# Experts ranked by row count on the chip, with one weight fetch each and blocks of 128 or 64 slots

## What is computed

```python
def _hier_moe(h, w_rg, b_rg, w_re, b_re, w1, w3, w2):
    ...
    g_top = jnp.argmax(g_logits, axis=-1)
    ...
    top_v, top_j = lax.top_k(e_in, TOP_K_EXPERTS)          # 2 of the 4 experts of the group
    w_sel = jax.nn.softmax(top_v, axis=-1) * gate_g
    e_id = g_top[:, None] * EXPERTS_PER_GROUP + top_j
    ...
    for e in range(N_EXPERTS):                              # 16
        he = jax.nn.silu(hf @ w1[e]) * (hf @ w3[e])
        y = y + combine[:, e:e + 1] * (he @ w2[e])
```

## Time and profile before

| | |
|---|---|
| median of three timed runs | 1888.61 us |
| span of the profiled execution | 1885.4 us |
| TensorE busy | 1815.4 us (96%) |
| VectorE busy | 1446.7 us (77%) |
| ScalarE busy | 982.6 us (52%) |
| GpSimd busy | 118.2 us (6%) |
| moved by DMA | 417.14 MB, mean 221 GB/s |

### The profile page before, as it was taken

One profiled execution on the slowest core, in us unless ns is written; L12 is line 12 of the kernel. 1 busy time (PEld: TensorE's weight loads), 2 busy tenths in 40 slices (PEclk: granted clock), 3 DMA queues, 4 the chain that ended last, 5 costly groups with the idle time before them and its releaser, 6 DMA issues.

```text
span 1885.4 us, 28170 instructions
## 1 busy us (share of the span) xinstructions
PE 1815.4 (96%) x10912; PEld 1597.0 (85%) x10912; DVE 1446.7 (77%) x1543; ACT 982.6 (52%) x932; POOL 118.2 (6%) x116
## 2 busy tenths in 40 slices
PE   7999999999999999999999999998998899999998
PEld 6888899998888788889999978886997777777876
DVE  7555786857877765567877687779588889999998
ACT  4444465534444454446464345443435456767774
POOL 1000000000000000000000000001000011212222
PEclk9999999999999999999999999998999999999999
DMA  6555455564777465545546557774432359999995
GB/s 250 190 188 196 161 179 179 201 224 144 280 252 259 157 216 185 200 156 181 199 164 245 176 186 279 248 260 144 140 136 90 103 185 373 367 373 391 389 385 217
DMA packets 61615, 417.14 MB, mean 221 GB/s; under 512 B 7288, under 2 KB 7664, under 8 KB 13648
## 3 DMA queue, kind: packets, MB, share of 16 engines
q1 hardware_dynamic: 51392, 369.19, 54.4%
q0 software_dynamic: 10112, 46.59, 7.3%
q10 hardware_dynamic: 16, 0.01, 0.0%
HBM read 405.79 MB, written 9.98 MB: 221 GB/s over the span
## 4 chain that ended last, share of the span: by engine, by line
PE 80%; DVE 11%; DVEq 3%; issue 3%; ACT 1%; ACTq 1%; DMA 0%; POOL 0%; POOLq 0%
PE ps L1916 14%; PE ps L1915 7%; PE ps L1900 7%; PE ps L1902 7%; PE ps L1901 7%; PE ps L2017 4%; PE ps L2018 4%; PE ps L2021 4%; PE ps L899 3%; PE ps L897 3%; PE ps L898 3%; PE ps L926 2%; PE ps L1913 2%; DVE wlo L2350 2%; PE ps L928 2%
## 5 line engine op out<-in xcount | busy, mean ns | idle before, releaser
L2350 DVE TENSOR_TENSOR wlo<-raw,whi 128x2048 fp32r<-128x2048 f32 x236 | 538.2, 2289 | 194.0 <-ACT whi L2182 191.2
L2182 ACT ACTIVATE whi<-raw 128x2048 fp32r<-128x2048 f32 x236 | 451.1, 1912 | 271.6 <-PE ps L1902 112.7
L1916 PE MATMUL ps<-xT,whi 128*128 128x512 f32 x1232 | 440.4, 397 | 0.0
L1915 PE MATMUL ps<-xT,wlo 128*128 128x256 f32 x1232 | 344.6, 280 | 0.1
L1916 PEld LDWEIGHTS ps<-xT,whi 128*128 128x128 f32 x1232 | 231.9, 188 | 47.6
L1900 PE MATMUL ps<-xT,whi 128*128 128x256 f32 x928 | 263.5, 284 | 2.0 <-DVE xT L2361 2.0
L1901 PE MATMUL ps<-xT,whi 128*128 128x256 f32 x928 | 263.2, 284 | 0.0
L1902 PE MATMUL ps<-xT,wlo 128*128 128x256 f32 x928 | 263.1, 284 | 0.0
L1915 PEld LDWEIGHTS ps<-xT,wlo 128*128 128x128 f32 x1232 | 233.0, 189 | 8.9 <-DVE xT L2369 1.0
L1544 DVE TENSOR_TENSOR wlo<-raw,whi 128x2048 fp32r<-128x2048 f32 x76 | 201.3, 2661 | 10.6 <-ACT whi L1124 9.9
L2206 ACT ACTIVATE rest<-ps 128x512 f32<-128x512 f32 x88 | 52.7, 599 | 251.9 <-PE ps L1916 251.9
(11 more groups left out here) (516 smaller groups left out, 3288.1 us busy)
## 6 DMA issues: line engine op xcount, KB each, us to landing
raw<-stream SPq DMA_DIRECT2D x236, 1024.0 KB, 4.9
raw<-experts SPq DMA_DIRECT2D x76, 1024.0 KB, 7.2
mod<-experts SPq DMA_DIRECT2D x38, 1024.0 KB, 6.7
adaraw<-ada POOLq DMA_DIRECT2D x24, 1024.0 KB, 5.1
yd<-lnrow POOLq DMA_DIRECT2D x17, 512.0 KB, 8.7
lnrow<-ln_g POOLq DMA_DIRECT2D x6, 512.0 KB, 4.8
lnrow<-ln_b POOLq DMA_DIRECT2D x6, 512.0 KB, 6.3
x_sb<-x SPq DMA_DIRECT2D x1, 1024.0 KB, 5.1
```

What stands on the lines that cost most here:

```text
L1915: nc.tensor.matmul(bank(b, T), wl, xThi[:, k, :], start=False, stop=False)
L1916: return nc.tensor.matmul(bank(b), wh, both, start=False, stop=k == KD - 1)
L2182: act_fn(whi[:, slot, :], raw[:, slot, :], ACT.Copy).then_inc(hi_done, 1)
L2350: v.tensor_tensor(wlo[:, slot, :], raw[:, slot, :], whi[:, slot, :].bitcast(F32), ALU.subtract).then_inc(lo_done, 1)
```

## The change

- Experts are ranked by their number of rows on the chip (`key`, `place_of`, `perm`, in `sort2`), largest first. Rank r can have at most min(256, 512 // (r + 1)) rows, which fixes when the kernel is built how many blocks an expert of that rank has, and of which width: ranks 0 and 1 two blocks of 128, rank 2 one of 128 and one of 64, ranks 3 to 6 one of 128, ranks 7 to 15 one of 64. `RANK_AT` is the rank of the expert at position q.
- Weights are fetched once for each expert, 96 units instead of 114; all blocks of an expert use them. Each expert's number is read from `emap`, so no fetch starts before the sort (`ev["sorted"]`).
- In a block of 64 the operand has the high parts in one half of its 128 columns and the low parts in the other; two matmuls (with the weights' high and low part) replace three. The gate and up rows are turned by 8 matmuls with `fold`, which adds high and low, then silu and product are made on turned rows, and output halves are added (`rows_out`).
- Column copies go from GpSimd to ScalarE (`columns`). Both gathers come before the first expert. Splits of the first four units come after all selections.
- Two banks of PSUM sets and two sets of hidden rows serve experts with two blocks. With two blocks, products wait until rows of the expert before the last are out of PSUM.
- Filler matmuls: 20 instead of 12 after ranks (`PLACE_FILL`), 12 new ones after the gathers (`FIRST_FILL`).
- Stored rows are no longer multiplied by `g2` on the way; `near_sum` multiplies both halves.

```diff
+def widths(q):
+    left = rows_at_most(RANK_AT[q])
+    out = []
+    while left > 0:
+        out.append(LIGHT if left <= LIGHT else SLOTS)
+        left -= out[-1]
+    return out
...
+RANK_AT = [0, 7, 8, 9, 1, 10, 11, 12, 2, 13, 14, 15, 3, 4, 5, 6]
...
         def sp_block2(sp):
-            for p in range(6 * BLOCKS):
+            for p in range(6 * EXPERTS):
...
+                if j == 0:
+                    if q == 0:
+                        sp.wait_ge(ev["sorted"], 1)
+                        expert = 0
+                    expert, last = sp.value_load(emap[0:1, q:q + 1], min_val=0, max_val=EXPERTS - 1), expert
...
-            columns(1)
-            columns(2)
-            for b in range(FAR):
-                store(b)
-                if b + 3 < BLOCKS:
-                    columns(b + 3)
+            for n in range(FAR):
+                store(n)
...
+                for n, m, width in BLOCKS_OF[q]:
+                    o = bank((G_BANK if j < 2 else U_BANK)[m])
...
+                        if width == SLOTS:
+                            h, lo = (xcur(n)[:, part, k, :] for part in range(2))
+                            mm(o, h, wh[:, rs], start=k == 0, stop=False)
+                            mm(o, h, wl[:, rs], start=False, stop=False)
+                            last = mm(o, lo, wh[:, rs], start=False, stop=k == KD - 1)
+                        else:
+                            both = light_columns(n, k)
+                            mm(o, both, wh[:, rs], start=k == 0, stop=False)
+                            last = mm(o, both, wl[:, rs], start=False, stop=k == KD - 1)
...
+            for c in range(BATCHES):
+                for group in range(8):
+                    gather(c, group)
+            idle(FIRST_FILL)
+            for q in range(EXPERTS + 1):
+                if q >= 1:
+                    turn_hidden(first_block(q - 1))
+                if q < EXPERTS:
+                    pe.wait_ge(ev["xcur"], last_block(q) + 1)
+                    if q >= 1:
+                        pe.wait_ge(silu_done, FFN_DONE + first_block(q - 1) + 1)
+                    if len(BLOCKS_OF[q]) > 1 and q > 0:
+                        pe.wait_ge(ev["y_left"], first_block(q) - 1)
+                        pe.wait_ge(ev["y_right"], first_block(q) - 1)
+                    product(q, 0)
+                    product(q, 1)
+                    if q == EXPERTS - 1:
+                        turn_shares()
+                if q >= 1 and len(BLOCKS_OF[q - 1]) > 1:
+                    turn_hidden(last_block(q - 1))
+                if q < EXPERTS:
+                    product(q, 2)
+                    product(q, 3)
+                if q >= 1:
+                    outputs(q - 1, 4)
+                    outputs(q - 1, 5)
...
+            for c in range(BATCHES):
+                for pair in range(4):
+                    select(c, pair)
+            columns(0)
+            for p in range(SPLITS):
+                expert_hi(p)
...
+            v.scalar_tensor_tensor(key, n_of, float(EXPERTS), down_from, ALU.mult, ALU.add)
...
+            v.tensor_tensor(sort2[:, :, :], across_q(key), down_q(key), ALU.is_gt)
...
+            for q in range(EXPERTS + 1):
+                two = q >= 1 and len(BLOCKS_OF[q - 1]) > 1
+                if q >= 1:
+                    turned_hidden(first_block(q - 1))
+                if two:
+                    product_rows(last_block(q - 1))
+                if q < EXPERTS:
+                    freed(q, 0)
+                    freed(q, 1)
+                if two:
+                    turned_hidden(last_block(q - 1))
...
+                if q < EXPERTS:
+                    freed(q, 2)
+                    product_rows(first_block(q))
+                    freed(q, 3)
...
+                if q >= 1:
+                    freed(q - 1, 4)
+                    for n, _, _ in BLOCKS_OF[q - 1]:
+                        rows_out(n)
+                    freed(q - 1, 5)
```

More of the change, by code:

```diff
@@ L884, in gather, with product @@
                 ins.then_inc(xT_ps, 1)
-            def product(b, j):
-                p = expert_unit(b, j)
+            def product(q, j):
+                p = expert_unit(q, j)
                 unit_split(pe, p)
                 wh, wl = splits[p % SPLITS]
-                o = bank(j // 2)
-                for r in range(4):
-                    k = 4 * (j % 2) + r
-                    h, lo = (xcur[b % 2][:, part * KD + k, :] if b else xsel[:, part, k, 0:SLOTS] for part in range(2))
-                    rs = slice(r * D_EXPERT, (r + 1) * D_EXPERT)
-                    mm(o, h, wh[:, rs], start=k == 0, stop=False)
-                    mm(o, h, wl[:, rs], start=False, stop=False)
-                    last = mm(o, lo, wh[:, rs], start=False, stop=k == KD - 1)
-                last.then_inc(used, 1)
@@ new lines, in product, with turn_hidden @@
+                last.then_inc(used, 1)
+            def turn_hidden(n):
+                _, m, width = BLOCK[n]
+                o = bank(T_BANK[m])
+                if n >= 1:
+                    pe.wait_ge(hlo_done, FFN_DONE + n)
+                if width == SLOTS:
+                    pe.wait_ge(hid_done, FFN_DONE + n + 1)
+                    for f in range(4):
+                        last = nc.tensor.transpose(o[:, f * P:(f + 1) * P], hide[:, f * P:(f + 1) * P], eye[:, :])
+                else:
+                    pe.wait_ge(silu_done, FFN_DONE + n + 1)
+                    pe.wait_ge(ev["ucopy"], LIGHT_NO[n] + 1)
+                    for a, rows_in_two in enumerate((gated, hide)):
+                        for f in range(4):
+                            c = (4 * a + f) * LIGHT
+                            last = mm(o[:, c:c + LIGHT], rows_in_two[:, f * P:(f + 1) * P], fold, start=True, stop=True)
@@ L1720, in dve_block2 @@
                 select(0, pair)
-            expert_lo(2)
             first_one_hot(1)
-            expert_lo(3)
+            block_offsets()
+            for pair in range(4):
+                select(1, pair)
+            for p in range(SPLITS):
+                expert_lo(p)
             def weights():
@@ new lines, in dve_block2 @@
+            for q in range(EXPERTS + 1):
+                two = q >= 1 and len(BLOCKS_OF[q - 1]) > 1
+                if q >= 1:
+                    turned_hidden(first_block(q - 1))
+                if two:
+                    product_rows(last_block(q - 1))
+                if q < EXPERTS:
+                    freed(q, 0)
+                    freed(q, 1)
+                if two:
+                    turned_hidden(last_block(q - 1))
+                if q == 1:
+                    steps_of_first_blocks()
+                elif q == 2:
+                    steps_of_second_blocks()
+                elif q == 3:
+                    choice_rows()
+                elif q == 4:
@@ L1785, in dve_block2 @@
[L1785 to L1793 removed]
+                elif 10 <= q < 10 + TT:
+                    far_shares(q - 10)
```

482 lines of the change are left out of this document (264 added, 218 removed).

## The result

| | before | after |
|---|---|---|
| median of 17 runs each | 1887.86 us (1887.32 to 1890.15) | 1892.87 us (1891.47 to 1894.73) |
| span of the profiled execution | 1885.4 us | 1892.8 us |
| mean granted clock of it | 0.992 | 0.980 |

The changed kernel takes 1.0026 of the time of the one before (95% interval 1.0019 to 1.0033): 5.0 us slower. The forecast was 5.6 us faster, with 1883.0 as the likeliest time.

The account below looks back on a forecast made before the run. TensorE (96% busy) bounds the kernel, VectorE within 5%, binding light experts. First product at 1546.9 plus iterations and tail ends at 1879.8, 5.6 us less; plus 3.2 from span to median gives 1883.0, range 1858 to 1898.

Parts of the forecast that it names:

- the term for the clock: At the first product: about 3.5 us at half speed after TensorE's wait behind its fillers, charged 1.75 us.
- tail: Last turn to end of span: 18.05 us before, plus 1.4 for two more multiplications on VectorE, so 19.45.
- rival 2: Expert stage: waits make the granted clock fall inside it, adding 19 us, to 1902; chance 0.18.
- the borders: Around two-block experts 4 and 8: waits of 6.5 us before their products and 3.1 before the second turn behind them.
- The removal and the additions: Expert stage: 39.6 us of splits, 55.8 of matmuls, 31 of stretching removed; 17.3 of turns added; net near 43 saved.
- the stretching of 1.74 per block: VectorE in each old block: splits beside GpSimd's column copy lose 1.74 us; 31 us go with the 18 copies.
- A light iteration: Iteration of an expert with one 64-wide block: VectorE needs 16.35 us and binds; TensorE needs only 13.0.
- A wide one: Iterations 13 to 15, experts with one 128-wide block: TensorE-bound, 17.2 us each, share turns of 0.44 extra.
- Two bounds: VectorE and ScalarE: 64-partition operations cost full (taken) or nothing, -8 to 0 us; ScalarE: strided 64-wide columns, 0 to +2.
- The start: Before the first product: weight fetches now wait for the sort, so it starts at 1546.9, 18.0 us later than before.
- Rival 1: Expert stage: VectorE runs ahead and TensorE stays the bound, timed 1851; holding in part, 1852 to 1876; chance 0.24.
- Rival 3: Expert stage: weight transfers bind the light experts, +6 to +9 us, 1889 to 1892; chance 0.08.

Follow-up runs that it names:

- e1_fill_waits: Kernel after with 134 more filler matmuls in TensorE's waits, no wait shortened: 1877.79 us, 0.9944 of the kernel before.
- e2: Kernel after with the high part of weight unit 0 made on ScalarE between the two batches of selections: 1888.10 us.
- e8: e7 with the first of expert 0's two column copies on VectorE and fewer fillers (10 before the first product, 3 before 64-wide turns): 1862.22 us.
- e4: Kernel before with only the column copies moved from GpSimd to ScalarE, ahead of the gate rows: 1894.07 us, 1.0027 of before.
- e10: e4 with the column copies later on ScalarE, at the end of a block's product units: 1880.32 us, 0.9960 of the kernel before.
- e3: Kernel after with the fillers of e1_fill_waits, but 22 instead of 41 before the first product, and the edit of e2: 1873.69 us.
- e6: e3 with the previous expert's output rows moved ahead of the last three splits before two-block experts, and no fillers there: 1866.25 us.
- e7: e6 with, in iterations 4 and 8, first-block turned rows and second-block gate/product rows ahead of output rows and last split, no second-turn fillers: 1861.63 us.
- e12: e7 with the up-row copy of 64-wide blocks on ScalarE instead of VectorE, and 2 fillers instead of 5 before their turns: 1857.55 us.

## Why the prediction was wrong

**The step that failed is the term for the clock.** The prediction charged 1.75 us, once, for half speed after the filler matmuls at the start. The trace shows 44 us at 0.50 inside the stage, and e1_fill_waits, which removes these and the 3.4 us at the second gather and takes no work away, is 15.1 us faster. The forecast's end of 1879.8 against the measured 1892.8 leaves 13.0; by iteration, forecast and measured:

| part | forecast | measured | clock |
|---|---|---|---|
| first product at | 1546.9 | 1548.92 | |
| 0 | 24.1 | 24.9 | 0.88 |
| 1, 2 and 3 | 52.3 | 51.9 | 1.00 |
| 4 | 32.6 | 34.8 | 0.90 |
| 5 | 22.7 | 24.45 | 0.93 |
| 6 and 7 | 29.4 | 29.5 | 1.00 |
| 8 | 28.8 | 30.8 | 0.89 |
| 9 | 22.1 | 25.7 | 0.87 |
| 10 to 12 | 49.4 | 52.6 | 0.82 in 11, 0.91 in 12 |
| 13 to 15 | 52.0 | 51.3 | 1.00 |
| tail | 19.45 | 18.0 | 1.00 |

(Lengths from the last output matmul of an iteration to the next, clocks from the windows from turn to turn.) The parts with a clock under 1.00 miss by 0.8, 2.2, 1.75, 2.0, 3.6 and 3.2, some 13.6 together. Those at 1.00 are met within 0.7, but for the tail.

**Why the term was too small.** The prediction had the mechanism as rival 2 and computed 1902 for it, but set against it: busy 14.96 of 20 at a clock of 1.00. It compared busy shares and didn't look at how the 5 idle us of that stretch are spread. The timeline of the kernel before shows that most of them lie in two waits:

```profile
1444.93 1.16 PE L785 MATMUL ps<-qkT 64*128 64x128 f32 x16 [2.03 <-ACT qkT L1053]
...
1456.79 1.09 PE L771 MATMUL ps<-eye,lnrow 128*128 128x128 f32 x8 [3.32 <-ACT lnrow L1076]
```

The second wait began at 1453.5, so the row that ended at 1456 stopped in the middle of it, and the next rows hold what came behind it: 0.50 from 1458 to 1468, of which the earlier trace rows show 1460 to 1466. The stretch that was held against the rival was the start of a case for it. The waits of the stage are of that size: 3.66, 3.39, 3.67, 3.39 and, at the start, 6.97. The prediction itself had forecast them (it named 6 at the start, 6.5 at the borders and 3.1 at the second turns) and then judged the clock by the busy share of a light expert. By the Trainium skill ("TensorE: Matmul & The Clock Gate", section on HAM oscillation) such waits cost the rate each time anew. The trace of the kernel after agrees for the waits of 3.39 and more, each with a stretch at 0.50.

**How much the falls cost.** Rival 2's 19 us were 15.1, so it had the mechanism right and its size somewhat too large. Of 44 us at 0.50, TensorE worked in 35, which lost 17.6, and the 3.4 us at the second gather lost 1.7. By iteration, the work lost and what e1_fill_waits got back were 2.1 and 2.1 in iteration 4, 1.5 and 1.5 in 5, 2.4 and 2.4 in 8, 3.4 and 3.2 in 9. In iteration 11 3.4 were lost but only 1.4 came back, since TensorE waits for VectorE there at either rate. And the fillers themselves made the light iterations 6 and 10 longer by 0.7 and 0.4.

**Which waits did it.** In the kernel after, waits of 3.39 and more were followed by 0.50 each time, and so were the 2.84 ahead of the second gather and the two of 1.90 and 1.91 at experts 10 and 11, the last one only after its turn had run at full speed. Waits of 1.71, 1.47 and 0.77 were not. The length alone doesn't decide it: in e2 the same wait of 1.71 was followed by 0.50, and waits of 2.75 (e2) and 2.51 (e8) ahead of the first product were not. What else decides was not tried.

**The removal and the additions.** These held. Two splits take 4.5 without the copy on GpSimd (e4, e10), so the stretching of 1.74 per block was real; e10 turned it into 7.7 us only, as a block of the kernel before is bound by TensorE at 17.0 next. A light iteration was forecast at 16.35 for VectorE plus routing steps, and takes 17.33 and 16.17. A wide one was forecast at 17.2 and takes 17.1 (51.33 for three). Two bounds can be closed: a 64-partition sum of 1024 columns costs VectorE 1.21, where two 512-column copies of 128 partitions take 1.29 together, so a narrow operation costs what a full one does, which is the end that was taken (beside it on ScalarE the evacuation takes 1.02); narrow column copies take 1.06.

**The start.** Forecast 18.0 later than before, measured 20.0, of which 1.3 lies in unchanged code ahead of it. The wait ahead of the first product was forecast at 6 and is 6.97. e2 shows that 5.1 us up to the first product were a matter of order: ScalarE's first high part needs no gather. It starts 31.3 after the logits were turned, and in e3, which has the same edit, 16.9.

**The borders.** Forecast right in place and cause, less so in size. At experts 4 and 8 TensorE waits 3.66 and 3.67 for rows that queue behind splits, and 3.39 before the second turn, forecast 3.1. The prediction allowed for them as given. e6 and e7 show that 12 us more than with fillers could be had by queue order: waits of an engine for something short that stands behind something long, which it doesn't need yet.

**The tail.** Forecast 1.4 longer for two more multiplications, measured equal, 17.98 against 18.05. The reading behind the forecast was wrong: VectorE had slack. The chain that ended last runs over TensorE in both kernels, whose matmuls with shares follow its last outputs without a wait (the chain in order of time, before and then after):

```profile
1875.28 6.88 PE ps L946 x16
```

```profile
1882.77 6.88 PE ps L1015 x16
```

VectorE waited 0.81 for them ahead of its last sums in the kernel before, and 0.17 in the kernel after: the two multiplications took up the slack.

**The rivals.** Rival 1, TensorE the bound and 1851 (its sum is 2 us too high: 277.8 us of matmuls and turns from 1546.9 end at 1824.7), is false for the kernel as it is: light iterations are VectorE's. e12, with the falls and most waits removed, reaches 1857.55, in the range of "in part it can hold" (1852 to 1876). Rival 3 is false: from 1560 to 1860 units land 4.7 to 10.1 us after issue, median 6.7; where the low part waits it is for ScalarE's high part, and the high part waits for TensorE, not for a transfer, even at 407 GB/s in a light iteration.

**Span and median.** In the profiles the miss is 13.0 us, in the medians 9.9. The 3.2 us by which the median of before lay over its profiled span were carried over to the kernel after, whose span and median differ by 0.1 only. In every run the timed figure is 1.6 to 1.8 above the span of the same execution; the rest was scatter between executions and no property of the kernel: the profiled execution of the kernel before lay at the lower end of its times, and that of the kernel after, 1894.60, at the upper end.

## What to carry to other kernels

When a change adds waits of several microseconds ahead of dense matmuls, price each twice: the wait, and the matmuls behind it at half the rate; judge it by a stretch of the old trace with waits of the same length, not with the same busy share, and read on past the wait, as the lower rate shows in the matmuls only behind it. First look for the short operation that queues behind a long one that TensorE doesn't need yet, and exchange the two; where no order helps, matmuls whose result nobody reads hold the clock in the wait. A copy moved to an engine with room is free only at a place in its queue where nothing that a fuller engine waits for stands behind it.

## What the runs showed of the hardware that was not expected

- A wait has its price again behind it, but only for the part of the half rate in which TensorE works: at the border to expert 4 a wait of 3.66 us brought 6.8 us at 0.50, of which 4.2 lay behind the wait, and cost 2.1 us; in iteration 9, where TensorE worked through all 6.8, it cost 3.2.
- 134 additional matmuls made the kernel 15.1 us faster. They are not free where they outlast the wait: in e1_fill_waits two light iterations became 0.7 and 0.4 us longer.
- The mean over a long stretch hides it. Iteration 4 reads 0.90, which looks harmless; the matmuls at its head started 0.43 apart instead of 0.23.
